# Attention of the first block: the values product of a differential unit ahead of the neighbourhood unit's two transpositions

## The chip, the cores and the metric

The kernel runs on one core of one Trainium2 chip. The metric is the device time of one execution in microseconds (us). The kernel before takes 4008.56 us (median of 3 runs, 4008.51 to 4011.54). Engine names in the profile: PE is TensorE's matmuls, PEld its weight loads, DVE is VectorE, ACT is ScalarE, POOL is GpSimd, SP is SyncE, which issues the DMAs.

## The reference, cut to what matters

Two transformer blocks run one after the other, of two layers each, on 512 tokens of width 1024. The change touches the first block only, in its two layers. Each layer of the first block mixes tokens in four ways, and two of them are attentions over 4 heads each:

```python
def diff_core(q, k, v, lam):
    s = jnp.einsum('bhcqd,bhckd->bhcqk', q, k).astype(jnp.float32) * (DIFF_QK ** -0.5)
    a = jax.nn.softmax(s, axis=-1)
    w = (a[:, :, 0] - lam * a[:, :, 1]).astype(v.dtype)
    return jnp.einsum('bhqk,bhkd->bhqd', w, v)
```

This is the differential attention: two softmaxes for a head, and the values are weighted by their difference. The neighbourhood attention (`na_attention_latent`) has one softmax per head, over a window of near tokens with a bias and over 256 context tokens, and then the same product with values. In layer 0 the 256 context tokens are queries too; their rows attend to the 256 context keys alone.

## The kernel before, in words

**Units.** `att_units` (L909) cuts a layer's attention into units of 128 queries and two softmaxes each. A differential unit ("diff") is one head with its two score maps; a neighbourhood unit ("na") is a pair of heads. They come in threes: diff of head 0, diff of head 1, then na of the group before. Layer 0 has 36 units, layer 1 has 24. Queries of kind "lat" have 768 keys (6 blocks of 128), queries of kind "ctx" 256 keys (2 blocks).

**What a unit needs.** Scores on PE (L1056) into PSUM banks 0 to 3; for na-lat units a bias by DVE (L1192) and a copy by ACT (L1292); the row extreme by DVE (L1203); the exponential by ACT (L1301), followed by a read of its row sum under the same line; then the weights: for a diff unit one DVE instruction (L1184) and a diagonal matrix by POOL (L1372), for an na unit two scalings by ACT (L1285). Next the weights are transposed on PE, blocks 0 to 2 into bank 4 and blocks 3 to 5 into bank 5 (L1071 for diff, where the transposition is a matmul with the diagonal, L1073 for na). DVE copies bank 4 to SBUF and ACT copies bank 5 (L1211 and L1310, into HC for diff and HL for na). A diff unit has one transposition, since its two maps are already joined; an na unit has two, `turn(u, 0)` and `turn(u, 1)`, and both use banks 4 and 5. For na-ctx units the first uses bank 4 alone and the second bank 5 alone. Last comes the product with values (`values`, L1091) into bank 6, which ACT copies out (L1317). A pair of diff units has one such product, with the second of them; an na unit has its own.

**The order.** Each engine has one written order. All engines run a software pipeline over steps `s`: step `s` issues the scores of unit `s`, the transposition of unit `s - 1` and the values of unit `s - 2`. "Beside" work goes into some steps as well (`item`, L1111): the Fourier and gated mixers of the layer (L1103, L1139, L1146, L1147, L1129) and modulation products (L399, L413). ACT's order inside a step matters here:

```python
if 1 <= s <= n and units[s - 1][1] == "na":
    take(s - 1, 0)          # ACT's copy of bank 5, first transposition
if s < n:
    exponential(s, 1)       # what scores(s + 1) waits for
```

Ahead of these lines ACT does `scaled(s - 1)` and `exponential(s, 0)`; after them the items, `mixed(s - 2)` (the copy of bank 6) and `take(s - 1, 1)`. DVE's order is: weights of `s - 1`, bias and row extremes of `s`, `take(s - 1, 0)` from bank 4, the items, `take(s - 1, 1)`.

**Waits on PE.** `turn(u, a)` waits for its weights (`soft_a ... "w"` for na) and for the copy that last emptied its bank (`turned_before`, L941). `values(u)` waits for both copies of its unit's transposed weights (L1081). `scores(s + 1)` waits for both exponentials of unit `s` (`scores_taken`, L925).

Of the kernel before, what the change touches and what calls it, by code (L numbers as in the profile page):

```python
# [165 lines left out]
def program(nc, d):  # L166
    ctx = ExitStack()
    with ctx:
# [45 lines left out]
        def C(name):  # L214
            a, n = CONST_AT[name]
            return cst[:, a:a + n]
# [6 lines left out]
        def bank(i):  # L223
            return ps[:, i, :]
# [164 lines left out]
        def tensor_mod_parts(e, w, li, i, pr, *free):  # L389


            w.wait_ge(silu_a.at(), silu_g.at(), *free)
            for b in range(2):
                wt = ada_buf(li, i + b)
                w.wait_ge(ada_landed(li, i + b))
                for r in range(2):
                    for q in range(4):
                        k = 4 * r + q
                        mm = e.matmul(pr[32 * q:32 * q + 32, 256 * b:256 * b + 256], silp[:, k, :], wt[:, k * 256:k * 256 + 256],  # L399
                                      start=r == 0, stop=r == 1)  # L400
                mm.then_inc(*mod_mm.up(li, i + b, "part"))
# [7 lines left out]
        def tensor_mod_sum(e, w, li, i, pr, *free):  # L409

            w.wait_ge(mod_a.at(li, i), (in_const, 16), *free)
            for j in range(4):
                mm = e.matmul(pr[:, 2 * j:2 * j + 2], modp[:, i // 2 % 2, 128 * j:128 * j + 128], C("sel"), start=True, stop=True)  # L413
            mm.then_inc(*mod_mm.up(li, i))
# [222 lines left out]
        def unit_of(l, kind, j=0):  # L637
            return next(p for p, u in enumerate(proj_units(l)) if u[0] == kind and u[2] == j)
# [5 lines left out]
        def pt_ready(l, kind, t):  # L644
            return lin_a.at(l, unit_of(l, kind), t // 2 * 2)
# [263 lines left out]
        def att_units(l):  # L909


            qts = [(i, "lat") for i in range(4)] + ([(i, "ctx") for i in range(2)] if l == 0 else [])
            groups = [(jt, *q) for jt in range(2) for q in qts]
            out = []
            for g in range(len(groups) + 1):
                if g < len(groups):
                    out += [(groups[g][0], "diff", hh, *groups[g][1:]) for hh in range(2)]
                if g:
                    out.append((groups[g - 1][0], "na", None, *groups[g - 1][1:]))
            return out  # L920
# [10 lines left out]
        def turns_of(l, u, a):  # L931

            jt, sort, hh, qi, kind = att_units(l)[u]
            if sort == "diff" and a:
                return []
            return [(range(0, 3), 4), (range(3, 6), 5)] if kind == "lat" else [(range(0, 2), 4 + (hh or a))]

        def turned(l, u, a, bk):
            return (wt_v if bk == 4 else wt_a).at(l, u, a)
# [10 lines left out]
        def has_values(l, u):  # L950
            return att_units(l)[u][2] != 0
# [7 lines left out]
        def values_before(l, u):  # L959

            return max((x for x in range(u) if has_values(l, x)), default=None)
# [28 lines left out]
        def last_diff(l, j):  # L990

            return max(u for u, x in enumerate(att_units(l)) if x[0] == j - 2 and x[1] == "diff")
# [44 lines left out]
        def tensor_attend(e, w, l):  # L1037
            units = att_units(l)
# [37 lines left out]
            def values(u):  # L1076
                jt, sort, hh, qi, kind = units[u]
                if not has_values(l, u):
                    return
                vb, vk, col = ([0, 1, 2, 3, 4, 5] if kind == "lat" else [4, 5]), *(("dv", 256) if sort == "diff" else ("nv", 512))  # L1080
                for x in (u - 1, u) if sort == "diff" else (u,):  # L1081
                    w.wait_ge(*(turned(l, x, a, bk) for a in range(2) for _, bk in turns_of(l, x, a)))
                before = values_before(l, u)
                if l == 0:
                    w.wait_ge(*(sub_a.at(l, j, "ln", 1) for j in (2, 3) if last_diff(l, j) + 4 <= u + 2))
                w.wait_ge(rot_v.at(l, unit_of(l, "dk", 1), "sin") if before is None else pv_a.at(l, before))
                for x, b in enumerate(vb):
                    w.wait_ge(pt_ready(l, vk, b))
                    for a in range(2):
                        c = col + (2 * jt + a) * 64  # L1090
                        mm = e.matmul(bank(6)[64 * a:64 * a + 64, 0:128], PT[:, b, c:c + 64], WT[sort][a][:, x * 128:x * 128 + 128], start=x == 0,  # L1091
                                      stop=x == len(vb) - 1)
                mm.then_inc(*pv_mm.up(l, u))

            def four_part(op, part, f, some):
                tts, n, _ = four(l, part)
                key, off = ((op, l, 0), 0) if part == 0 else (("fc", l, 1), 0 if op == "fc" else 512)
                wt = ring_buf(key, 2048 if part == 0 else 1024)
                w.wait_ge(landed(key))
                for x, t in enumerate(tts):  # L1100
                    if x in some:
                        w.wait_ge(pt_ready(l, "f", t))
                        mm = e.matmul(bank(7)[:, 0:n], PT[:, t, f * 128:f * 128 + 128], wt[:, off + x * n:off + x * n + n],  # L1103
                                      start=x == 0, stop=x == len(tts) - 1)
                return mm

            def free7(it):
                x = bank7.index(it)
                w.wait_ge(beside_taken(l, bank7[x - 1]) if x else norm_a.at("inv", (l, "mix"), len(segs_of(0)) - 1))

            def item(it):  # L1111
                pr = bank(7)
                if it[0] == "half":
                    free7(it[1:])
                    four_part(*it[1:], (0, 1))
                if it[0] not in ON_BANK7:
                    return
                free7(it)
                if it[0] == "parts":
                    tensor_mod_parts(e, w, it[1], it[2], pr)  # L1120
                elif it[0] == "sum":
                    tensor_mod_sum(e, w, it[1], it[2], pr)
                elif it[0] == "sqs":
                    j = it[1]
                    w.wait_ge(sub_a.at(l, j, "sq"))
                    if l == 0:
                        w.wait_ge(pv_a.at(l, values_before(l, min(last_diff(l, j) + 2, len(units)))))
                    for out, c, d_ in sub_psum(l):
                        mm = e.matmul(out, C("b64"), sub_buf(l, j)[:, c:d_], start=True, stop=True)  # L1129
                    mm.then_inc(*sub_mm.up(l, j))  # L1130
                elif it[0] == "gm":
                    _, f, (a, b) = it
                    wt = ring_buf(("ws", l), 512)
                    w.wait_ge(landed(("ws", l)))
                    for g in (2 * f, 2 * f + 1):
                        for t in range(a, b):
                            w.wait_ge(loc_v.at(l, "v", t))
                            r0 = g % 2 * 64
                            mm = e.matmul(pr[r0:r0 + 64, (t - a) * 128:(t - a) * 128 + 128], PT[:, t, 768 + g * 64:768 + g * 64 + 64],  # L1139
                                          wt[:, g * 128:g * 128 + 128], start=True, stop=True)  # L1140
                    mm.then_inc(*loc_mm.up(l, *it))
                elif it[0] == "fp":
                    _, part, f = it
                    n = four(l, part)[1]
                    w.wait_ge(loc_a.at(l, "fc", part, f), loc_v.at(l, "fs", part, f, "out"))
                    e.matmul(pr[:, 0:n], C("cd"), LB[:, 0:n], start=True, stop=False)  # L1146
                    e.matmul(pr[:, 0:n], C("sd"), LB[:, 512:512 + n], start=False, stop=True).then_inc(*loc_mm.up(l, *it))  # L1147
                else:
                    four_part(*it, (2, 3) if it[1] == 0 else (0, 1)).then_inc(*loc_mm.up(l, *it))

            n = len(units)
            for s in range(len(plan)):
                if s < n:
                    scores(s)
                for it in plan[s]:
                    item(it)
                if 1 <= s <= n:
                    turn(s - 1, 0)
                if 2 <= s <= n + 1:
                    values(s - 2)  # L1160
                if 1 <= s <= n:
                    turn(s - 1, 1)
# [2303 lines left out]
```

## Time and profile before

| | |
|---|---|
| median of 3 runs | 4008.56 us (4008.51 to 4011.54) |
| the profiled execution: its time, its span | 4007.92 us, 4006.1 us |
| PE busy over the span | 97% |
| DVE, ACT, POOL busy | 44%, 36%, 29% |
| mean granted TensorE clock | 0.988 of full |
| attention of layer 0 | from about 209 to 405 us of the span |
| attention of layer 1 | from about 1259 to 1408 us |

The span is the time from the program's first to its last instruction; the execution's time is 1.8 us longer. PE has the largest busy share, and the chain of work that ended last lies on PE for 86% of the span.

### The profile page before, as it was taken

How to read it: one execution, taken by the hardware profiler on the slowest of the kernel's cores; microseconds unless marked ns; L12 is line 12 of the kernel's file. 1: busy time of each engine (PE TensorE's matmuls, PEld its weight loads, DVE VectorE, ACT ScalarE, POOL GpSimd, SP SyncE). 2: the span in 40 equal slices, each digit the busy share in tenths (PEclk: the TensorE clock that was granted, in tenths of full speed). 3: DMA queues.
4: the chain of work that ended last, by engine and by line, in shares of the span. 5: the costliest groups of instructions: out<-in, count | busy, mean ns of one | idle time of the engine just before them, and what ended most of it. 6: DMA issues, size and time to landing. Idle time of an engine off the chain costs nothing.

```text
span 4006.1 us, 60979 instructions
## 1 busy us (share of the span) xinstructions
PE 3886.2 (97%) x26104; PEld 3087.3 (77%) x26104; DVE 1748.8 (44%) x2693; ACT 1423.3 (36%) x2258; POOL 1153.7 (29%) x689
## 2 busy tenths in 40 slices
PE   8999999999999899999999999999999999999998
PEld 6966778888877578887677778788876777887886
DVE  3366332323354643435755423334358464234333
ACT  3256332322233643332343333333324433334332
POOL 0010121222211023331332235333323322353333
PEclk9989999999999999999999999999999999999999
DMA  5014132323211022222111022222221111232221
GB/s 216 32 53 156 64 121 94 123 91 104 89 57 51 22 87 95 90 90 79 50 57 39 23 80 99 98 95 93 92 74 58 38 39 39 91 104 85 95 100 68
DMA packets 61356, 323.55 MB, mean 81 GB/s; under 512 B 6176, under 2 KB 6304, under 8 KB 36256
## 3 DMA queue, kind: packets, MB, share of 16 engines
q1 hardware_dynamic: 61088, 319.65, 23.0%
q8 instruction: 207, 3.39, 0.3%
q14 instruction: 61, 0.50, 0.0%
HBM read 317.53 MB, written 2.10 MB: 80 GB/s over the span
## 4 chain that ended last, share of the span: by engine, by line
PE 86%; DVE 5%; issue 3%; ACT 3%; POOL 1%; DMA 1%; SPq 0%; DVEq 0%; POOLq 0%; ACTq 0%
PE ps L1557 52%; PE ps L1568 4%; PE ps L735 3%; PE ps L766 3%; PE ps L2625 3%; PE ps L2259 2%; PE ps L1056 1%; PE ps L3127 1%; PE ps L338 1%; PE ps L1091 1%; DMA adab<-in_wada 1%; PE ps L2700 1%; PE ps L2722 1%; PE ps L2720 1%; PE ps L1071 1%
## 5 line engine op out<-in xcount | busy, mean ns | idle before, releaser
L1949 DVE SCALAR_TENSOR_TENSOR ftmp<-ps,vec,ftmp 128x511 f32<-128x511 f32 (+2 forms) x440 | 301.6, 694 | 342.8 <-ACT ftmp L1903 224.7
L1529 POOL TENSOR_TENSOR PWL<-ring,PWH 128x1024 fp32r<-128x1024 f32 (+2 forms) x114 | 260.5, 2285 | 655.4 <-ACT PWH L1515 655.4
L1529 POOL TENSOR_TENSOR WL<-ring,WH 128x1024 fp32r<-128x1024 f32 (+3 forms) x102 | 227.5, 2230 | 574.0 <-ACT WH L1515 557.4
L1515 ACT ACTIVATE PWH<-ring 128x1024 fp32r<-128x1024 f32 (+2 forms) x216 | 211.5, 982 | 465.6 <-PE ps L1557 422.2
L1515 ACT ACTIVATE WH<-ring 128x1024 fp32r<-128x1024 f32 (+3 forms) x160 | 158.5, 993 | 578.9 <-PE ps L1557 545.4
L1557 PE MATMUL ps<-FH,WH 128*128 128x512 f32 x1008 | 308.1, 360 | 0.0
L1557 PE MATMUL ps<-FL,WH 128*128 128x512 f32 x1008 | 304.5, 356 | 0.0
L1557 PE MATMUL ps<-FH,WL 128*128 128x512 f32 x1008 | 303.4, 355 | 0.0
L1529 POOL TENSOR_TENSOR PW3L<-ring,PW3H 128x1024 fp32r<-128x1024 f32 (+2 forms) x90 | 204.3, 2270 | 253.3 <-ACT PW3H L1515 253.2
L1522 DVE TENSOR_TENSOR PWL<-ring,PWH 128x1024 fp32r<-128x1024 f32 (+2 forms) x102 | 125.3, 1230 | 347.7 <-ACT PWH L1515 347.5
L1557 PEld LDWEIGHTS ps<-FH,WH 128*128 128x128 f32 x1008 | 166.3, 188 | 38.8 <-issue 9.9
L1972 POOL TENSOR_TENSOR ftmp<-ftmp 128x512 f32<-128x512 f32 (+1 forms) x88 | 126.3, 1435 | 230.6 <-DVE ftmp L1949 230.3
L1557 PEld LDWEIGHTS ps<-FH,WL 128*128 128x128 f32 x1008 | 166.2, 188 | 28.8
L1557 PEld LDWEIGHTS ps<-FL,WH 128*128 128x128 f32 x1008 | 165.9, 188 | 27.8
L1515 ACT ACTIVATE PW3H<-ring 128x1024 fp32r<-128x1024 f32 (+2 forms) x106 | 104.1, 982 | 229.9 <-PE ps L1557 218.7
L1557 PE MATMUL ps<-FH,PWL 128*128 128x512 f32 x432 | 170.2, 394 | 0.0
L1557 PE MATMUL ps<-FL,PWH 128*128 128x512 f32 x432 | 169.3, 392 | 0.0
L1557 PE MATMUL ps<-FH,PWH 128*128 128x512 f32 x432 | 167.6, 388 | 0.0
L1522 DVE TENSOR_TENSOR WL<-ring,WH 128x1024 fp32r<-128x1024 f32 (+3 forms) x58 | 68.2, 1176 | 217.2 <-ACT WH L1515 217.1
L1954 DVE TENSOR_TENSOR AL<-ftmp,AH 128x512 fp32r<-128x512 f32 (+1 forms) x88 | 66.8, 759 | 211.7 <-ACT AH L1913 211.7
L1913 ACT ACTIVATE AH<-ftmp 128x512 fp32r<-128x512 f32 (+1 forms) x88 | 60.3, 686 | 265.9 <-POOL ftmp L1972 265.9
L1557 PE MATMUL ps<-AH,WH 128*128 128x512 f32 x494 | 150.9, 360 | 0.0
(625 smaller groups left out, 9864.0 us busy)
## 6 DMA issues: line engine op xcount, KB each, us to landing
ring<-in_wup SPq DMA_DIRECT2D x88, 1024.0 KB, 4.8
adab<-in_wada SPq DMA_DIRECT2D x56, 512.0 KB, 5.3
ring<-in_wgate SPq DMA_DIRECT2D x24, 1024.0 KB, 4.8
ring<-in_wdown SPq DMA_DIRECT2D x24, 896.0 KB, 4.7
ring<-in_win SPq DMA_DIRECT2D x18, 1024.0 KB, 4.8
ring<-in_wout SPq DMA_DIRECT2D x16, 1024.0 KB, 4.8
ring<-in_wada SPq DMA_DIRECT2D x14, 1024.0 KB, 4.9
ring<-in_wdown SPq DMA_DIRECT2D x12, 1024.0 KB, 5.0
```

Of the source, the lines that this page charges most:

```text
L735: mm = e.matmul(pr[:, c:c + n], ww[:, k, :], h[part][:, k, :], start=start, stop=stop)
L766: mm = e.matmul(out, x, ww[:, k, :], start=kk == 0 and n == 0, stop=kk == 7 and n == 2)
L1515: e.activation(wh, view, ACT.Copy).then_inc(*whi_a.up(L, n))
L1522: e.tensor_tensor(wl, view, wh.bitcast(F32), SUB).then_inc(*wlo_v.up(L, n))
L1529: e.tensor_tensor(wl, view, wh.bitcast(F32), SUB).then_inc(*wlo_g.up(L, n))
L1557: mm = e.matmul(out[:, c:c + h.shape[1]], ww[:, k, :], h, start=at == 0 and p == 0, stop=at == K - 1 and p == 2)
L1568: mm = e.matmul(outs[j][:, c:c + h.shape[1]], ww[:, k, :], h, start=k == order[0] and ww is ws[j][0] and part == 0, stop=k == order[-1] an ...
L1949: e.scalar_tensor_tensor(out=dst, in0=src, scalar=conv_cols(L, ch, a), in1=dst, op0=MUL, op1=ADD).then_inc(*(ffn_v.up(L, "tap", x, j, c) i ...
L1954: e.tensor_tensor(lo, z_slot(L, x, 0)[:, 0:N], hi.bitcast(F32), SUB).then_inc(*ffn_v.up(L, "low", x))
L1972: e.tensor_tensor(zg, zg, zv, MUL).then_inc(*ffn_g.up(L, x))
L2259: mm = e.matmul(bank(6), ww[:, k, :], t, start=k == 0 and i == 0, stop=k == 7 and i == 2)
L2625: mm = e.matmul(front_bank(what, pp), ww[:, k, :], h, start=k == 0 and x == 0, stop=k == 7 and x == 2)
```

## The change

In a step whose transposed unit is na and whose values unit is diff, PE's product with the values is issued ahead of `turn(s - 1, 0)` instead of between `turn(s - 1, 0)` and `turn(s - 1, 1)`. The same instructions are issued. The order of the other engines is as before.

```diff
                 for it in plan[s]:
                     item(it)
+                ahead = 2 <= s <= n and units[s - 1][1] == "na" and units[s - 2][1] == "diff"
+                if ahead:
+                    values(s - 2)
                 if 1 <= s <= n:
                     turn(s - 1, 0)
-                if 2 <= s <= n + 1:
+                if 2 <= s <= n + 1 and not ahead:
                     values(s - 2)
                 if 1 <= s <= n:
                     turn(s - 1, 1)
```

The condition holds in 11 steps of layer 0 (s = 5, 8, 11, ..., 35) and in 7 of layer 1 (s = 5, 8, ..., 23).

## Rows read from the trace of the kernel before

**Rows 1.** Windows, one per layer's attention: us, busy of each engine, clock, DMA.
```profile
core 0: us, PE busy (x) PEld busy (x) DVE busy (x) ACT busy (x) POOL busy (x), PEclk, DMA share, GB/s
209.00:409.00 200.00, 181.22 (x1394) 120.90 (x1394) 128.01 (x255) 116.05 (x275) 23.19 (x31) 0.91 0.28 104
1259.00:1409.00 150.00, 129.56 (x944) 88.73 (x944) 101.49 (x172) 89.18 (x189) 16.10 (x21) 0.93 0.12 44
```

**Rows 2.** Groups by line, na transpositions, layer 0 then 1: busy, mean ns | idle before.
```profile
L1073 PE MATMUL ps<-cst,ar 128*128 128x128 f32 x112 | 18.4, 295 | 2.8 <-ACT ar L1285 2.8
...
L1073 PE MATMUL ps<-cst,ar 128*128 128x128 f32 x96 | 15.9, 308 | 13.3 <-ACT ar L1285 11.9 <-DVE HL L1211 1.4
```

**Rows 3.** Timeline, layer 1, s = 8: start us, length us, engine, line, tiles, count [idle before].
```profile
1309.52 0.82 PE L1073 MATMUL ps<-cst,ar 128*128 128x128 f32 x6
...
1310.27 1.53 PE L1091 MATMUL ps<-HC,ar 128*64 128x128 f32 x24
1310.38 0.49 ACT L1310 ACTIVATE HL<-ps 128x384 f32<-128x384 f32 x1 [0.24 <-PE ps L1073]
1310.77 0.90 ACT L1301 ACTIVATE ar<-ps,small 128x768 f32<-128x768 f32 x1
1311.55 0.20 ACT L1301 ACTIVATION_READ_ACCUMULATOR ar<-ps,small 128x1 f32 x1
1311.73 0.88 PE L1073 MATMUL ps<-cst,ar 128*128 128x128 f32 x6
...
1312.32 0.56 DVE L1211 COPY HL<-ps 128x384 f32<-128x384 f32 x1 [1.71 <-PE ps L1073]
1312.54 1.56 PE L1056 MATMUL ps<-ar 32*128 32x512 f32 x8
1312.65 0.49 ACT L1310 ACTIVATE HL<-ps 128x384 f32<-128x384 f32 x1 [0.52 <-PE ps L1073]
```

**Rows 4.** Timeline, layer 0, s = 11: the exponential of a context unit.
```profile
277.25 0.47 ACT L1301 ACTIVATE ar<-ps,small 128x256 f32<-128x256 f32 x1
```

**Rows 5.** Timeline, layer 1, s = 23: PE waits for DVE's copy.
```profile
1394.66 0.88 PE L1073 MATMUL ps<-cst,ar 128*128 128x128 f32 x6 [2.28 <-ACT ar L1285]
...
1397.53 0.55 DVE L1211 COPY HL<-ps 128x384 f32<-128x384 f32 x1
...
1398.23 1.49 PE L1073 MATMUL ps<-cst,ar 128*128 128x128 f32 x6 [0.53 <-DVE HL L1211]
```

**Rows 6.** Timeline, layer 1, s = 17.
```profile
1360.26 0.47 ACT L1310 ACTIVATE HC<-ps 128x384 f32<-128x384 f32 x1
1361.64 1.24 PE L1073 MATMUL ps<-cst,ar 128*128 128x128 f32 x6 [2.18 <-ACT ar L1285]
1362.81 2.79 PE L1091 MATMUL ps<-HC,ar 128*64 128x128 f32 x24
1363.20 0.47 ACT L1310 ACTIVATE HL<-ps 128x384 f32<-128x384 f32 x1
1363.57 0.90 ACT L1301 ACTIVATE ar<-ps,small 128x768 f32<-128x768 f32 x1
1366.34 1.56 PE L1056 MATMUL ps<-ar 32*128 32x512 f32 x8
```

**Rows 7.** Windows around the start of that step's transposition; columns as in Rows 1.
```profile
1354.00:1361.00 7.00, 5.24 (x40) 3.20 (x36) 5.38 (x10) 4.22 (x12) 0.60 (x1) 1.00 0.02 5
1362.20:1365.20 3.00, 3.00 (x26) 2.67 (x26) 0.64 (x2) 2.35 (x6) 0.00 (x0) 0.50 0.00 0
```

**Rows 8.** Timeline, layer 1, s = 14.
```profile
1345.24 1.54 PE L1073 MATMUL ps<-cst,ar 128*128 128x128 f32 x6 [3.77 <-ACT ar L1285]
...
1347.20 0.90 ACT L1301 ACTIVATE ar<-ps,small 128x768 f32<-128x768 f32 x1
...
1349.77 1.56 PE L1056 MATMUL ps<-ar 32*128 32x512 f32 x8
```

**Rows 9.** Timeline, layer 0, s = 20, a context unit's two transpositions.
```profile
320.49 0.44 PE L1073 MATMUL ps<-cst,ar 128*128 128x128 f32 x2 [1.52 <-ACT ar L1285]
...
321.67 0.89 ACT L1301 ACTIVATE ar<-ps,small 128x768 f32<-128x768 f32 x1
...
324.19 1.20 PE L1056 MATMUL ps<-ar 32*128 32x512 f32 x4
```

## The prediction

> **What bounds the kernel now.** I read the page first: PE is busy 97% of the span and holds 86% of the chain that ended last, so only what PE waits for can be won, and whatever PE is made to wait for is lost. The change touches two stretches, together 350 us of 4006; in them PE is busy for 181.22 of 200 us and 129.56 of 150 us, at 0.91 and 0.93 of its clock [rows 1]. The groups by line say where PE idles ahead of the transpositions that the change moves: 2.8 us in layer 0 and 13.3 us in layer 1, nearly all for ACT's scaling L1285 [rows 2]. The timeline then shows two kinds of step. In a **packed** step PE goes from the first transposition to the product, to the second transposition, to the next scores without a pause [rows 3]. In a **waiting** step it stands for 1.5 to 3.8 us ahead of the first transposition, and then has the product still to do [rows 6, 8, 9]. Of the 18 changed steps five wait: s = 20 of layer 0 and s = 14, 17, 20, 23 of layer 1. Eleven are packed, all with a latent na unit: s = 5, 8, 11, 14, 23, 26, 29, 32 of layer 0 and 5, 8, 11 of layer 1. The last two are s = 17 and 35 of layer 0, with a context na unit.
>
> **What the change costs in a packed step.** Nothing is added or removed. The product takes 1.46 us from start to start (1310.27 to 1311.73), the scores begin 3.02 us after the first transposition [rows 3]. Before, that product covered two things: the emptying of banks 4 and 5 between the two transpositions, and ACT's copy of bank 5 with the exponential behind it, which the next scores need. After it, the first transposition starts some 1.40 us later (the step begins with the product; 1.46 less 0.06 that the shorter first transposition shows), and both follow uncovered.
>
> The first is the bank. DVE's copy starts 0.59 us after a transposition that follows a product (1311.73 to 1312.32) and takes 0.56 [rows 3]; from the end of such a copy to PE's start are 0.15 (1398.08 to 1398.23) [rows 5]. So the second transposition starts 1.30 after the first instead of 0.81: a pause of 0.49 us. With it the scores come at 1.40 + 1.30 + 0.81 = 3.51, which is 0.49 later. ACT's copy of bank 5 is ready before the second half needs it.
>
> The second is the exponential. ACT's copy starts 0.92 after the transposition, the exponential 0.39 after the copy, and it ends with its read 0.98 later (1310.77 to 1311.75) [rows 3]; with 0.15 to PE the scores start at 1.40 + 0.92 + 0.39 + 0.98 + 0.15 = 3.84 at the earliest, 0.82 later than 3.02. Where the next unit is a context unit, the exponential takes 0.47 in place of 0.90 [rows 4], and the bank decides with 0.49.
>
> Seven packed steps have a latent unit next (s = 5, 8, 23, 26 of layer 0; 5, 8, 11 of layer 1) and four a context unit (11, 14, 29, 32 of layer 0). At s = 23 of layer 0 a pause of 0.43, one of those in the 2.8 us [rows 2], takes up half, which leaves about 0.3. Sum of the losses: 6 x 0.82 + 0.3 + 4 x 0.49 = 7.2 us. PE runs on without a pause behind these steps, so I pass the loss on whole. Its lower bound is nothing but the bank in all eleven, 11 x 0.49 less 0.4 = 5.0 (if ACT's work is ahead of where these rows have it), its upper bound the whole cover lost, 11 x 1.46 = 16; I take the worked value, since each term is a row.
>
> **The page that speaks against it.** The trace shows the second transposition directly behind a DVE copy with PE idle 0.53 us [rows 5]. The Trainium skill (Perfetto Trace Analysis, Matmuls) says that independent matmul groups should rotate through different PSUM banks, so that emptying one lies beside the next group's matmuls; here the product in bank 6 was the rotation between two users of banks 4 and 5. That rule gives the sign of the packed steps and no figure; without it the sum is the same.
>
> **What it gains in a waiting step.** The product can start when ACT has copied the diff unit's weights. At s = 17 of layer 1 that copy ends at 1360.73, PE at 1360.88; 1.46 later, at 1362.34, the transposition starts, past the 1361.64 at which it began before. ACT's copy was at 1363.20 and now can't start before 1363.26; exponential, read and scores follow at 1363.65, 1364.63 and 1364.78, against 1366.34: 1.56 us won [rows 6]. That holds at full clock. Before, the clock fell from 1.00 to 0.50 (2.4 to 1.2 GHz) behind the pause of 2.18, and the product took 2.79 us in place of 1.53 [rows 3, 6, 7]. With a pause of 1.4 left, the fall may still come; then the product's end and the transposition run at the slow level (1.24 us and more for it) and about 0.6 is won. So 0.6 to 1.6, and I take 1.2. The step at s = 20 has the same pattern 16.5 us later: another 1.2.
>
> At s = 14 the exponential starts at 1347.20 behind ACT's own queue and stays there; the scores could start at 1348.33 against 1349.77: 1.4 [rows 8]. At s = 20 of layer 0 likewise, 321.67 + 0.98 + 0.15 = 322.80 against 324.19: 1.4 [rows 9]; context transpositions use a bank each, so nothing is lost there. At s = 23 the second transposition waits for DVE's copy at 1397.53, which stands behind DVE's own work: 0 [rows 5]. The gains: 2 x 1.2 + 1.4 + 1.4 = 5.2, between 4.0 and 6.4 (plus 0.4 at s = 23 if its transposition runs at full clock). The other two steps with context units (s = 17, 35) I cost at nothing: banks apart, no wait ahead.
>
> **Other queues.** DVE's copy of the first transposition moves 1.4 us later in a packed step, and with it an item behind it; the diff weights L1184 come some 0.5 to 1.1 later, which a score product and an item of 1 to 2 us on PE cover, except at s = 5 of layer 0, where I allow 0.2. ACT's copy of bank 6 comes earlier. POOL waits only for DVE's weights. SP's loads wait for items, which move by the same tenths, and no DMA is on the path here (share 0.28 and 0.12) [rows 1].
>
> **The sum.** 7.2 + 0.2 - 5.2 = +2.2 us on the profiled execution's 4007.92, so 4010.1. That execution lies 0.6 below the median 4008.56; from the median it would be 4010.8. I say 4010.5.
>
> **Rivals.** A: *the clock decides against the change*. Each packed step now has pauses of 0.49 and 0.33; if the clock falls to 1.2 GHz behind them, a product costs 2.79 - 1.53 = 1.26 more [rows 3, 6]. In all eleven that is 14 us, 4024; over the bound of a measurement from five falls on. For it: layer 0 already runs at 0.91 [rows 1], and behind the pause of 1.52 in rows 9 the clock fell too. Against: the pauses are half of the smallest in those rows. Chance 0.08.
> B: *the losses drown*. If a later pause on PE takes up what the packed steps lose (PE idles 18.8 and 20.4 us in the two stretches [rows 1]), only the gains stand: -5.2, so 4003. Against: the pauses follow from score products, which move along. Chance 0.15.
> C: *the change does nothing where it should*: the product isn't ready when PE idles, the waiting steps stay, the losses stand: +7.4, so 4016. Against: the copy it needs ends 0.9 us before the transposition starts [rows 6]. Chance 0.12.
> The forecast, gains and losses near each other, has 0.65.
>
> **How the numbers follow.** Forecast alone: losses 5.0 to 8, gains 4.0 to 6.8, so -1.8 to +4, and 1.5 for the spread of the runs: 4006 to 4014. With most of B and C: 4004 to 4016. A measurement can tell 0.2%, about 8 us, from no change: below 4000.5 is faster, above 4016.6 slower. Faster needs B with full gains and more: 0.03. Slower is A and the tail of C: 0.09. The same: 0.88.
>
> **What would show it.** Right: L1073's idle for L1285 in layer 1 falls from 11.9 to some 6 us; a new idle for DVE L1211 of about 0.49 stands ahead of ten or eleven second transpositions (5 us in all), and one for ACT L1301 of about 0.3 ahead of the scores in the latent packed steps; the layer 0 stretch grows by 3 to 4 us and layer 1's shrinks by 1 or 2. Wrong: if the scores of a packed step still start 3.0 us after its start, if the exponential isn't late, or if the granted clock of the two stretches falls below 0.91 and 0.93 [rows 1].

## The result, and the profile after

The changed kernel takes **4016.91 us** (median of 15 runs, 4010.47 to 4027.18). The kernel before, run beside it, takes 4005.96 (15 runs, 3998.20 to 4011.54). The ratio is 1.0027, with a 95% interval of 1.0020 to 1.0035: slower by 8 to 14 us. The forecast was 4010.5 with a range that ended at 4016. It missed: the change costs more than the range allowed for, and it lies beyond the 0.2% that I had called no change.

The page of the changed kernel: span, busy times, granted clock in 40 slices.

```profile
span 4015.0 us, 60976 instructions
...
PE 3888.9 (97%) x26104; PEld 3088.3 (77%) x26104; DVE 1751.1 (44%) x2693; ACT 1421.6 (35%) x2258; POOL 1152.8 (29%) x689
...
PEclk9989999999999999999999999999999999999999
```

The page alone tells nothing of the cause: the instructions are the same, and the shares too. The windows of the two stretches, and one inside the second; columns as in [rows 1]:

```profile
209.00:415.00 206.00, 182.91 (x1410) 121.91 (x1409) 128.83 (x255) 115.80 (x275) 23.13 (x31) 0.93 0.28 101
1265.00:1418.00 153.00, 131.89 (x944) 89.57 (x944) 102.66 (x172) 87.35 (x189) 15.99 (x21) 0.92 0.12 43
...
1406.00:1415.50 9.50, 7.85 (x42) 5.65 (x44) 1.12 (x2) 3.56 (x7) 0.00 (x0) 0.50 0.01 2
```

The windows are a little wider than those of [rows 1], so I measured both stretches from their first score product to the first weight product behind them. Layer 0 grew from 195.5 to 199.6 us and layer 1 from 147.8 to 151.4. I had expected layer 0 to grow by 3 to 4 and layer 1 to shrink by 1 or 2. That layer 0 comes near it is partly chance: in a second pair of traces (below) it grew from 192.6 to 198.4, and layer 1 from 146.2 to 147.9. The third row is a stretch at the end of layer 1 that ran wholly at 0.50 of the clock; before there were 3.4 us of that kind in the same place.

The groups by line, na transpositions (L1073) and the score products that wait (L1056), changed kernel, layer 0 and then layer 1. DVE's copy is now L1214, ACT's scaling L1288, the exponential L1304:

```profile
L1056 PE MATMUL ps<-ar 32*128 32x512 f32 x64 | 20.9, 729 | 7.4 <-ACT ar L1304 6.6 <-ACT ar L845 0.8
L1073 PE MATMUL ps<-cst,ar 128*128 128x128 f32 x112 | 17.1, 284 | 4.6 <-DVE HL L1214 3.3 <-ACT ar L1288 1.2
...
L1073 PE MATMUL ps<-cst,ar 128*128 128x128 f32 x96 | 16.6, 315 | 8.3 <-DVE HL L1214 5.0 <-ACT ar L1288 2.9 <-ACT HL L1313 0.3
L1091 PE MATMUL ps<-HC,ar 128*64 128x128 f32 x192 | 14.1, 302 | 5.1 <-issue 5.1
```

Against [rows 2]: the idle for ACT's scaling in layer 1 fell from 11.9 to 2.9, but 5.1 of it has only moved ahead of the product (L1091). New are the waits for DVE's copy, 3.3 us (eight times 0.41) in layer 0 and 5.0 in layer 1, where the old order had none and 1.4. The scores' wait for the exponential is 6.6 in layer 0 and was 4.0, as the same view of the kernel before shows:

```profile
L1056 PE MATMUL ps<-ar 32*128 32x512 f32 x64 | 20.6, 722 | 4.8 <-ACT ar L1301 4.0 <-ACT ar L845 0.8
```

The timeline of a packed step, changed kernel, layer 1, s = 8; it answers to [rows 3]:

```profile
1316.55 1.53 PE L1091 MATMUL ps<-HC,ar 128*64 128x128 f32 x24
...
1318.01 0.88 PE L1073 MATMUL ps<-cst,ar 128*128 128x128 f32 x6
1318.60 0.56 DVE L1214 COPY HL<-ps 128x384 f32<-128x384 f32 x1 [2.04 <-PE ps L1073]
1318.93 0.49 ACT L1313 ACTIVATE HL<-ps 128x384 f32<-128x384 f32 x1 [1.86 <-PE ps L1073]
...
1319.30 0.85 PE L1073 MATMUL ps<-cst,ar 128*128 128x128 f32 x6 [0.41 <-DVE HL L1214]
1319.31 0.90 ACT L1304 ACTIVATE ar<-ps,small 128x768 f32<-128x768 f32 x1
...
1320.10 0.20 ACT L1304 ACTIVATION_READ_ACCUMULATOR ar<-ps,small 128x1 f32 x1
...
1320.44 1.56 PE L1056 MATMUL ps<-ar 32*128 32x512 f32 x8 [0.29 <-ACT ar L1304]
```

Both pauses stand where they were forecast: 0.41 for the bank (forecast 0.49) and 0.29 for the exponential (forecast 0.33). From the first transposition to the scores it takes 2.43 us; I had 3.84 - 1.40 = 2.44. The rule of the Trainium skill (Perfetto Trace Analysis, Matmuls) on rotating PSUM banks agrees with this trace: the two transpositions now directly follow each other on the same banks, and 0.41 us of PE idle stand between them.

### The profile page after: what moved, and what is told of

Same layout as the page of the kernel before. It is cut to its first block, busy times and chain, and to the rows that moved or that the text cites. A ratio compares the mean times of both kernels' runs of the same rounds, so it can differ in the third digit from the quotient of the medians.

```text
span 4015.0 us, 60976 instructions
## 1 busy us (share of the span) xinstructions
PE 3888.9 (97%) x26104; PEld 3088.3 (77%) x26104; DVE 1751.1 (44%) x2693; ACT 1421.6 (35%) x2258; POOL 1152.8 (29%) x689
## 4 chain that ended last, share of the span: by engine, by line
PE 86%; DVE 5%; issue 3%; ACT 3%; POOL 1%; DMA 1%; SPq 0%; DVEq 0%; POOLq 0%; ACTq 0%
PE ps L1560 52%; PE ps L1571 4%; PE ps L735 3%; PE ps L766 3%; PE ps L2628 3%; PE ps L2262 2%; PE ps L1056 2%; PE ps L3130 1%; PE ps L338 1%; PE ps L1091 1%; DMA adab<-in_wada 1%; PE ps L2703 1%; PE ps L2725 1%; PE ps L2723 1%; PE ps L1071 1%
```

## The experiments

Each was timed beside the kernel before on the same chip. The runs of one kernel spread widely (the kernel before: 3997 to 4019 us around 4006.6), so no median settles a term of 1 us. What settles it is the time from one step's score products to the next step's, read from the trace of each kernel, with the time at 1.2 GHz inside in brackets. (Other steps are left out. s = 21 of layer 0 and s = 15 of layer 1 are not changed themselves; each follows a changed step.)

```
us (of these at 1.2 GHz)
step     before      before 2    after       after 2     e1_packed   e8_swap     e6_between  e9_before_fill
L0 s=8    6.33 (0)    6.33 (0)    7.30 (0)    7.30 (0)    7.30 (0)    6.94 (0)    6.14 (0)    6.33 (0)
L0 s=11   5.81 (0)    5.82 (0)    6.42 (0)    6.42 (0)    6.43 (0)    6.42 (0)    6.10 (0)    5.82 (0)
L0 s=14   8.34 (3.4)  6.64 (0)    8.90 (3.4)  8.89 (3.4)  8.83 (3.4)  8.89 (3.4)  8.38 (3.4)  6.65 (0)
L0 s=20   7.84 (3.2)  6.45 (0)    6.45 (0)    6.45 (0)    7.81 (3.2)  7.88 (3.4)  6.45 (0)    6.45 (0)
L0 s=21   4.67 (0.2)  4.57 (0)    6.11 (3.4)  6.10 (3.4)  4.70 (0.2)  4.60 (0)    4.57 (0)    4.57 (0)
L1 s=8    6.33 (0)    6.33 (0)    7.30 (0)    7.30 (0)    7.30 (0)    6.94 (0)    6.14 (0)    6.33 (0)
L1 s=14   9.86 (3.4)  9.97 (3.4)  8.38 (0)    8.38 (0)   10.59 (6.8) 10.55 (6.8) 10.83 (6.8)  8.41 (0)
L1 s=15   4.82 (0)    4.82 (0)    4.57 (0)    6.09 (3.4)  4.82 (0)    4.82 (0)    4.71 (0)    4.82 (0)
L1 s=17   8.43 (3.4)  8.43 (3.4)  8.38 (3.4)  6.95 (0)    8.40 (3.4)  8.43 (3.4)  6.82 (0)    6.82 (0)
L1 s=20   8.56 (3.4)  6.95 (0)    8.17 (3.4)  6.95 (0)    6.95 (0)    6.95 (0)    8.54 (3.4)  6.95 (0)
tail     16.56 (3.4) 16.23 (3.4) 19.81 (10.2) 17.51 (3.4) 16.2 (3.4)  16.3 (3.4)  16.2 (3.4)  16.00 (0)
```

"Before 2" and "after 2" are a second execution of each of the two kernels (below); the tail runs from the scores of s = 23 in layer 1 to the first weight product, L437.

**Half of the change: the packed steps alone.**

```diff
-                ahead = 2 <= s <= n and units[s - 1][1] == "na" and units[s - 2][1] == "diff"
+                ahead = s in ((5, 8, 11, 14, 23, 26, 29, 32), (5, 8, 11))[l]
```

> The product goes ahead in the eleven packed steps alone (s = 5, 8, 11, 14, 23, 26, 29, 32 of layer 0 and 5, 8, 11 of layer 1). Both theories: the scores behind each latent packed step come about 0.96 us later (0.3 at s = 23 of layer 0) and behind each of the other four about 0.6, in all 8.0 us, so 1.0020 of the kernel before. T1 (waits only): the changed kernel's other seven steps then give something back, and this kernel is slower than the changed one. T2 (clock): those seven give nothing or cost, and this kernel is faster than the changed one by 1 to 4 us.

Measured: 4012.20 against 4006.24, ratio 1.0017 (1.0008 to 1.0026), so 3 to 10 us slower. The packed steps of its trace are those of the changed kernel to 0.01 us, apart from s = 14 and 23 of layer 0 (0.07 and 0.03 us shorter) and s = 32, where the clock fell in this trace and not in that one. The changed kernel had 1.0027 in its own comparison, so the other seven steps seem to cost something and not to give back; the two intervals overlap, so the times alone don't show it.

**The other half: the waiting steps alone.**

```diff
+                ahead = s in ((20,), (14, 17, 20, 23))[l]
```

> The product goes ahead in the five waiting steps alone (s = 20 of layer 0; 14, 17, 20, 23 of layer 1). T1 (waits only): 4 to 5 us faster than before, as the forecast's gains had it (0.9988). T2 (the clock falls on what is left of the pauses and the moved product no longer keeps it up): 0 to 3 us slower than before, since s = 17 and 20 give 0.1 to 0.4 each in the trace of the changed kernel and s = 23 costs some 3.

Measured: 4004.11 against 4006.24, ratio 1.0000 (0.9991 to 1.0010). The gain of 5.2 is not there. Its trace has 6.12 (3.4) at s = 21 of layer 0, 8.38 (0) at s = 14 of layer 1, 8.32 (3.4) and 8.22 (3.4) at s = 17 and 20, and 19.75 us with 10.2 at 1.2 GHz in the tail.

**The last waiting step alone.**

```diff
+                ahead = (l, s) == (1, 23)
```

> The product goes ahead in one step alone, s = 23 of layer 1. T1 (waits only): no difference, at most 0.5 us faster, since the second transposition waits for DVE's copy either way. T2 (clock): 2 to 4 us slower than before; a longer stretch at half clock lies over the last transpositions and products of layer 1.

Measured: 4008.32 against 4006.24, ratio 1.0009 (1.0000 to 1.0018); its tail takes 17.44 us against 16.2 to 16.6 of the old order. I had costed this step at nothing. The timeline of the changed kernel shows why (TensorE, layer 1, s = 23 and behind it):

```profile
1400.14 1.53 PE L1091 MATMUL ps<-HC,ar 128*64 128x128 f32 x24 [1.50 <-issue]
1401.60 0.88 PE L1073 MATMUL ps<-cst,ar 128*128 128x128 f32 x6
1404.52 0.85 PE L1073 MATMUL ps<-cst,ar 128*128 128x128 f32 x6 [2.05 <-DVE HL L1214]
...
1406.83 1.54 PE L1073 MATMUL ps<-cst,ar 128*128 128x128 f32 x6 [1.45 <-ACT ar L1288]
1408.30 2.83 PE L1091 MATMUL ps<-HL,ar 128*64 128x128 f32 x24
1411.95 1.51 PE L1073 MATMUL ps<-cst,ar 128*128 128x128 f32 x6 [0.82 <-DVE HL L1214]
```

The product no longer lies between the two transpositions, so PE has three pauses within 8.2 us (1.50, 2.05, 1.45; the old order has 2.28 and 0.53 at that step, [rows 5]), and from 1405.6 on all that follows runs at 1.2 GHz, up to 1415.8.

**Work against the pauses.** The suspicion was now that the waiting steps' time hangs on the clock and not on the order. To test it PE gets matmuls in its pauses whose result nobody reads. `busy(k)` issues k of them, each two records of the trace and some 0.94 us (three take 2.84).

```diff
+            def busy(k):
+                w.wait_ge(sub_a.at(1, 2, "ln", 0))
+                for _ in range(k):
+                    e.matmul(bank(7), C("ident"), C("cos1"), start=True, stop=True)
...
+                if l == 1 and s in (17, 20, 23):
+                    busy(3)
```

Here and at s = 24 three, and four ahead of the second transposition of s = 23, on top of the changed kernel:

> The changed kernel with idle PE time of layer 1's last steps filled by extra matmuls of 128x128 by 512 columns into bank 7, whose result nobody reads: 3 ahead of the product at s = 17, 20 and 23, 4 between the two transpositions of s = 23, 3 ahead of the first of the last unit and 1 ahead of its second (17 in all, 0.43 us each by L1147 in the trace). T1 (waits only): no better than the changed kernel, up to 1 us slower. T2 (clock): no stretch at half clock there, and 5 to 7 us faster than the changed kernel.

(The edit has 16 of them, not 17: none stands ahead of the last unit's second transposition.)

Measured: 4015.87 against 4006.24, ratio 1.0020 (1.0010 to 1.0031). From s = 14 of layer 1 to the end of its stretch the clock held, but the test was spoilt by its size: three take 2.84 us, and s = 17 takes 8.16 us where it takes 6.95 with the clock up and none added. So a second one, on top of the changed kernel, with one at s = 17, 20, 23, 24, one behind the product of s = 14 and two between the transpositions of s = 23:

> As the run with 17 extra products, which turned out to be two matmul instructions each (2.84 us for three of them) and to delay the real product by 1.28 us; now few enough to end before the real work is ready: 1 ahead of the product at s = 17, 20, 23 of layer 1, 1 ahead of the first transposition at s = 14, 2 between the two of s = 23, 1 ahead of the last unit's (0.94 us each). T1 (waits only): like the changed kernel. T2 (clock): no half clock in layer 1's attention behind its first microseconds; at s = 17 and 20 the next scores begin 1.5 us earlier than before, 5.3 us after the end of the last scores; the stage of layer 1 is 5 to 7 us shorter than in the changed kernel (151.4), the time 5 us under it.

Measured: 4014.59 against 4007.63, ratio 1.0015 (1.0004 to 1.0026). The layer 1 stretch is 144.8 us (151.4 and 147.9 in the two traces of the changed kernel), with s = 17 at 6.81, s = 20 at 6.95 and a tail of 16.00. The losses of the packed steps remain. The ratio is 0.0012 under the changed kernel's 1.0027, near the expected 5 us, but the intervals overlap.

**Other work as the cover.** In the packed steps the product goes ahead, and the step's items, which PE has to do anyway, go between the two transpositions:

```diff
-                for it in plan[s]:
-                    item(it)
+                if s not in between:
+                    for it in plan[s]:
+                        item(it)
+                if s in ahead or s in between:
+                    values(s - 2)
                 if 1 <= s <= n:
                     turn(s - 1, 0)
+                if s in between:
+                    for it in plan[s]:
+                        item(it)
```

> In the eleven packed steps the order is product, first transposition, beside items, second transposition (before: items, transposition, product, transposition); all other steps as before. T1 (the product covered the emptying of banks 4 and 5 and ACT's copy; items of 1 to 3 us cover it as well): no pause for DVE's copy or the exponential, and the pauses ahead of the items (1.97, 1.04, 0.89, 0.82, 0.68, 0.27 in the trace of before) shrink: 4 to 8 us faster than before. Rival (what costs is the later first transposition itself, through DVE and ACT): 3 to 8 us slower than before, as the packed steps alone were.

Measured: 4004.07 against 4007.63, ratio 1.0000 (0.9988 to 1.0011); the expected gain is not there. The timeline of TensorE, layer 1, s = 8, in this kernel:

```profile
1307.75 1.53 PE L1091 MATMUL ps<-HC,ar 128*64 128x128 f32 x24
1309.21 0.88 PE L1073 MATMUL ps<-cst,ar 128*128 128x128 f32 x6
1309.92 1.88 PE L1103 MATMUL ps<-ring,ar 128*128 128x512 f32 x4
1311.64 0.82 PE L1073 MATMUL ps<-cst,ar 128*128 128x128 f32 x6
1312.39 1.56 PE L1056 MATMUL ps<-ar 32*128 32x512 f32 x8
```

Both pauses of the changed order are gone (6.14 us for the step, against 7.30 and 6.33). The cover can thus be replaced. But in other steps the item had also covered the time until ACT had copied the product's weights, and the pause now stands ahead of the product: 0.75 us at s = 11 of layer 0 (6.10 us for the step, 5.81 before), 0.71 at s = 26 (7.22 and 6.43) and 2.25 at s = 32, where the clock stayed down for 6.8 us (9.86 for the step; 7.24 before, with a fall, and 6.08 without). So layer 0 takes 197.7 us (195.5 and 192.6 in the two traces of before) and layer 1 146.2 (147.8 and 146.2), and the steps give back what the others won. The 6.8 us at 1.2 GHz at s = 14 of layer 1 aren't of this edit, which leaves that step alone: they stand in e1_packed and e8_swap too.

**That order, with the waiting steps ahead as well** (s = 20 of layer 0; 14, 17, 20 of layer 1, without 23):

```diff
+            between = ((5, 8, 11, 14, 23, 26, 29, 32), (5, 8, 11))[l]
+            ahead = ((20,), (14, 17, 20))[l]
```

> The order of the run before this one in the packed steps, and the product ahead in the waiting steps s = 20 of layer 0 and 14, 17, 20 of layer 1 (not 23). T1 (waits only): 3 to 5 us faster than the run before this one. T2 (clock takes back what the waiting steps win): within 1.5 us of the run before this one.

Measured: 4009.14 against 4007.63, ratio 1.0004 (0.9993 to 1.0015). The gain of 3 to 5 us isn't there: it is 5 us above the run before this one by the medians and 1.6 by the ratios, with intervals that overlap. Its layer 1 stretch is short, 142.7 us, and its layer 0 stretch 197.8, together 340.5 (343.3 and 338.8 in the two traces of before), yet the whole is not faster. Its profiled execution took 4015.69, so that one lost its time outside the two stretches, where 48.9 us ran at 1.2 GHz and 43.1 in the first trace of before. I can't tell more from it.

**The exponential taken by itself.** As in the packed steps alone, and ACT does the exponential ahead of its copy of bank 5 (`late` moves the call behind or ahead of it):

```diff
-                if 1 <= s <= n and units[s - 1][1] == "na":
+                late = units[s - 1][1] == "diff" or s in ((5, 8, 11, 14, 23, 26, 29, 32), (5, 8, 11))[l] if 1 <= s <= n else None
+                if late is False:
```

> The packed-only kernel with ACT's exponential of the next unit put ahead of its copy of bank 5 in those steps. If the exponential behind that copy is what makes the latent packed steps lose 0.96 and not 0.6, the pause ahead of the next scores (0.29, for ACT L1301's read) goes in the seven latent steps and each loses 0.6; the pause of 0.42 ahead of the second transpositions stays. Rival (only the bank counts): no change, 0.96 each.

Measured: one execution, 4011.25. The timeline of layer 1, s = 8, in this kernel:

```profile
1311.47 1.53 PE L1091 MATMUL ps<-HC,ar 128*64 128x128 f32 x24
...
1311.88 0.89 ACT L1304 ACTIVATE ar<-ps,small 128x768 f32<-128x768 f32 x1
...
1312.93 0.88 PE L1073 MATMUL ps<-cst,ar 128*128 128x128 f32 x6
...
1314.22 0.85 PE L1073 MATMUL ps<-cst,ar 128*128 128x128 f32 x6 [0.41 <-DVE HL L1214]
...
1315.01 1.56 PE L1056 MATMUL ps<-ar 32*128 32x512 f32 x8
```

The exponential now lies beside the product and the scores follow without a pause. The step takes 6.94 in place of 7.30, so the exponential is 0.36 of the 0.97 lost, and 0.61 stay with the bank; the steps with a context unit next, where the bank alone decides, lose the same 0.61 with or without it (L0 s = 11). This is one trace, but steps without a fall repeat to 0.01 us in the two traces of either kernel.

**The kernel before with products in its pauses, in its own order.** Two at s = 14, 17, 20 and 23 of layer 1 ahead of the first transposition, one at s = 24:

```diff
+                if l == 1 and s in (17, 20, 23, 24):
+                    busy(1 if s == 24 else 2)
+                ahead = False
...
+                if (l, s) == (1, 14):
+                    busy(2)
```

> The kernel before, its order untouched, with extra products of 0.94 us each in PE's pauses of layer 1's last steps: 2 ahead of the first transposition at s = 14, 17, 20, 23 and 1 ahead of the last unit's. T2a (the order wins nothing where the clock is up; all of a waiting step's gain was the comparison of a product at half clock with one at full clock): at s = 17 and 20 the next scores begin 5.3 us after the last ones end, as they do in the changed kernel with extra products (5.26, 5.39), against 6.88 and 7.0 before; layer 1's stage is 141 to 143 us (147.8 before); the time 3 to 6 us under the kernel before. T1 (the order wins 1.5 us in each even at full clock): 6.8 us there and a stage of 146 or more.

Measured: 4000.42 against 4006.57, ratio 0.9989 (0.9978 to 1.0000). This is the run that decides. The order is that of before, and s = 14 and 17 still come down from 9.86 and 8.43 to 8.41 and 6.82; at s = 17 the next scores begin 5.26 us after the last ones end, as expected if the order wins nothing in the step. The window over s = 15 to 24 and the timeline of s = 17 in this kernel:

```profile
1345.00:1399.00 54.00, 49.22 (x402) 32.98 (x402) 37.08 (x64) 35.79 (x79) 3.63 (x6) 1.00 0.00 1
```

```profile
1354.66 1.99 PE L1154 MATMUL ps<-cst 128*128 128x512 f32 x4
1356.90 0.88 PE L1073 MATMUL ps<-cst,ar 128*128 128x128 f32 x6 [0.26 <-ACT ar L1297]
1357.72 1.53 PE L1091 MATMUL ps<-HC,ar 128*64 128x128 f32 x24
1359.18 0.88 PE L1073 MATMUL ps<-cst,ar 128*128 128x128 f32 x6
```

The clock is 1.00 throughout; the product takes 1.53 where it took 2.79 [rows 6]. The layer 1 stretch is 142.9 us, 4.9 less than in the first trace of before and 3.3 less than in the second.

**The same with the waiting steps ahead** (s = 20 of layer 0; 14, 17, 20 of layer 1), one product each at 14, 17, 20 and 24, two at 23:

```diff
+                if l == 1 and s in (17, 20, 23, 24):
+                    busy(2 if s == 23 else 1)
+                ahead = s in ((20,), (14, 17, 20))[l]
```

> The product ahead only at s = 20 of layer 0 and 14, 17, 20 of layer 1, with extra products in the pauses that are left (1 at s = 14, 17, 20, 2 at s = 23, 1 ahead of the last unit's). T2a: the same stage of layer 1 as the run before this one within 0.7 us, 5.3 us between the scores. T1: 3 to 4 us shorter than the run before this one.

Measured: 4002.06 against 4006.57, ratio 0.9984 (0.9972 to 0.9996); layer 1 143.5 us. Both are faster than the changed kernel, and than the one before, the first of them at the edge of its interval. Between their times the runs show no difference. The traces show a small one: this run has one fall, at s = 15 of layer 1 (6.04 us in place of 4.57), and where neither has a fall the product ahead saves nothing in the waiting step itself and 0.25 us in the step behind it.

**Both kernels once more**, unchanged, one execution each.

> The kernel before again, for a second look at where the clock falls in its attention stages. T2 (falls depend on where the pauses lie): falls behind the pauses of L1073 at s = 14, 17, 20, 23 of layer 1 again, within one of the first trace's four, and both stages within 3 us of 195.5 and 147.8.

> The changed kernel again. If the step costs are of its order and not of chance, the gaps ahead of the second transpositions (0.42) and the scores (0.29) repeat to 0.02 us; stage lengths within 3 us of 199.6 and 151.4, the clock half at the tail of layer 1 again.

Measured: 4001.21 and 4016.15. The packed steps repeat to 0.01 us where the clock is the same in both traces, and so do the pauses of 0.41 and 0.29. For the kernel before, the falls came at three of the four places and the stretches (192.6 and 146.2) lie within 3 us, as expected. For the changed one, layer 0 does (198.4), but layer 1 takes 147.9 and not 151.4, with 3.4 us at 1.2 GHz in its tail and not 10.2. The falls of the clock do not repeat: s = 14, 20 and 29 of layer 0 and s = 20 of layer 1 in the kernel before, s = 17 and 20 of layer 1 in the changed one, ran at full clock this time, and the changed one fell at s = 15 of layer 1 instead. The kernel before, layer 1, s = 20, TensorE:

```profile
1370.59 1.56 PE L1056 MATMUL ps<-ar 32*128 32x512 f32 x8
1374.46 0.88 PE L1073 MATMUL ps<-cst,ar 128*128 128x128 f32 x6 [2.31 <-ACT ar L1285]
1375.27 1.53 PE L1091 MATMUL ps<-HC,ar 128*64 128x128 f32 x24
1376.73 0.88 PE L1073 MATMUL ps<-cst,ar 128*128 128x128 f32 x6
1377.54 1.56 PE L1056 MATMUL ps<-ar 32*128 32x512 f32 x8
```

## Why the prediction was wrong, step by step

**The losses of the packed steps: right in mechanism; in sum too, partly by luck.** Forecast 7.4 us (7.2 and 0.2). The eleven steps of the two first profiles differ by 0.66, 0.97, 0.61, 0.56, 0.33 and 0.82 (L0 s = 5 to 26), 0.54 (s = 29), 0.03 (s = 32) and 0.96, 0.97, 0.96 in layer 1: 7.4 us. (For s = 29 and 32 the value before is one of the same order at full clock, 5.71 and 6.08; at s = 14 both had a fall.) Four of the seven latent steps lose 0.97 and not 0.82, which makes up for s = 5 (0.66 for 0.82 and 0.2) and s = 32. The bank and the exponential were as worked out; the 0.06 that I had set off for a shorter transposition isn't saved, and the product starts 0.09 later behind the item than the transposition did. The single steps were less alike than my two classes: s = 32 lost nothing, since PE waited for ACT there in the old order too. The packed steps alone confirm the sum (ratio 1.0017, about 6.8 us).

**The gains of the waiting steps: the step that failed.** "0.6 to 1.6, and I take 1.2", twice, and 1.4 twice: 5.2 us. At equal clock the gain in these steps is **0**, and 0.6 us in all in the steps behind them. The rows had it. At full clock the old order needs 3.02 us from the first transposition to the scores [rows 3], so from 1361.64 the scores of s = 17 would have come at 1364.66. The new order brings them, by my own working, at 1364.78. I compared that with 1366.34, a number that held a product at 1.2 GHz, and took the difference of the clock for a gain of the order. The mechanism is the same one that I had counted in the packed steps: the product ahead starts 0.8 us earlier than the transposition could, and the bank and exponential laid bare behind it cost just that. At s = 20 of layer 0, where the transpositions share no bank, it is the exponential alone: the pause of 1.52 us ahead of the first transposition [rows 9] became one of 1.47 ahead of the next scores. The traces show it at full clock in both orders: 6.45 and 6.45 (L0 s = 20), 8.41 and 8.38 (L1 s = 14), 6.95 and 6.95 (s = 20). Only the step behind each waiting step of layer 1 gains, 4.57 in place of 4.82 us: a pause of 0.27 ahead of its transposition, for DVE's weights, is gone (at s = 16 a part of that, 0.13, is given back).

What remains is the clock. In its first trace the changed order leaves a pause of 1.36 us in place of 2.18 at s = 17 and of 1.50 in place of 2.28 at s = 23, and the clock fell all the same. The timeline of the changed kernel, TensorE, layer 1, s = 17, answers to [rows 6]:

```profile
1365.17 1.56 PE L1056 MATMUL ps<-ar 32*128 32x512 f32 x8
1368.09 2.83 PE L1091 MATMUL ps<-HC,ar 128*64 128x128 f32 x24 [1.36 <-issue]
1370.85 1.14 PE L1073 MATMUL ps<-cst,ar 128*128 128x128 f32 x6
1372.41 0.85 PE L1073 MATMUL ps<-cst,ar 128*128 128x128 f32 x6 [0.42 <-DVE HL L1214]
1373.55 1.56 PE L1056 MATMUL ps<-ar 32*128 32x512 f32 x8 [0.29 <-ACT ar L1304]
```

The product again takes 2.83. The falls must be counted over the steps behind as well, for some only moved there. At s = 20 of layer 0 no trace with the new order has a fall, but six of seven have one at s = 21, behind the pause that the order put ahead of the scores. The changed kernel there, first the timeline of TensorE, then a window from 1.0 us behind that pause, columns as in [rows 1]:

```profile
327.10 0.84 PE L1073 MATMUL ps<-cst,ar 128*128 128x128 f32 x4
329.42 2.02 PE L1056 MATMUL ps<-ar 32*128 32x512 f32 x8 [1.47 <-ACT ar L1304]
```

```profile
330.38:333.79 3.41, 3.41 (x13) 2.40 (x10) 2.34 (x3) 1.40 (x3) 0.00 (x0) 0.50 0.00 0
```

Each waiting step with the two steps behind it, over all traces without added products in that layer:

```
us, mean (traces)    old order, falls     new order, falls     both at full clock
L0 s=20 to 22        15.5 (7), in 3       16.2 (7), in 6       14.9 and 14.9
L1 s=14 to 16        18.4 (6), in 6       16.7 (4), in 1       16.5 and 16.4
L1 s=17 to 19        16.0 (6), in 5       15.6 (4), in 3       14.8 and 14.6
L1 s=20 to 22        15.7 (6), in 3       15.3 (4), in 2       14.9 and 14.6
```

(The 16.5 is of the kernel with added products, e9_before_fill; no other has the old order there without a fall.) The gain is 1.8 us on average, and not 5.2: 0.6 of it is the order's and the rest is clock, 1.6 won at s = 14 of layer 1 and 0.7 lost in layer 0. These are few traces, so the share of the clock is rough.

**The tail, costed at 0 and up to 0.4 won: wrong in sign.** It costs 1.2 us where the clock falls once and 3.3 where it stays down for 10.2 us. At full clock it takes 16.00 us in either order; only the kernels with added products show that.

**A step costed at 0 that costs a little.** s = 35 of layer 0: from its scores to the first weight product it takes 9.29 us at full clock in the new order and 9.03 in the old.

**The sum.** Losses 7.4, waiting steps -1.8, tail +2.3 (18.6 us on average in the four traces with the new order at s = 23, 16.3 in six with the old one), s = 35 +0.3: 8.2 us, against a forecast of 2.2 and a measured 8 to 14. The stretches give a like sum another way. Four traces have layer 0 wholly in the old order (192.5 to 195.5 us, mean 193.3) and four wholly in the changed one (198.4 to 202.5, mean 200.1); layer 1 takes 147.0 in the two traces of before and 149.7 in the two of after. That is 6.8 + 2.7 = 9.5 us, inside the interval.

The 6.8 of layer 0 is 1.3 more than its steps account for (4.5 packed, 0.7 at s = 20 to 22, 0.3 at s = 35), and that is the clock. Ahead of s = 14's item stands a pause of 1.97 us for ACT, in both orders alike, and the step has a fall in 2 of 6 traces with the old packed order and in 8 of 8 with the product moved (8.4 to 8.9 us in place of 6.6, where I have counted 0.56). But at s = 29 it is 3 of 6 and 0 of 8, and at s = 32 5 of 6 and 6 of 8. From s = 5 on the four old traces have 5, 2, 2 and 2 falls in layer 0, the four changed ones 3, 2, 4 and 4. So the change moves falls; whether it makes more of them in layer 0 these traces don't show, and no run was made to test it.

**The rivals.** C came nearest: the losses stand whole and the waiting steps give almost nothing, 4016. Its reason was wrong, though: the product was ready, and PE did start it early (the idle for the scaling fell to 2.9, not 6). A, that the clock decides, was right about the cause and wrong about the place: in none of the packed steps' traces did the clock fall directly behind a pause of 0.41 or 0.29; it fell in the tail, at s = 21 of layer 0, and more often at s = 14 there. (At the waiting step s = 14 of layer 1 it fell in two traces, r_after and e10_wait_fill, 1.0 and 1.3 us behind the last of four pauses: 1.49 in the one and 0.43 in the other, then 0.43, 0.26 or 0.25, and 0.42.) Its argument against, that the new pauses are half of the smallest with a fall, rested on the rows alone: the same trace has falls at pauses of 1.04 and 0.89 us, at s = 29 and 32 of layer 0. B is refuted by the packed steps alone.

## What to carry to other kernels

Compare two orders of the same work only at the same granted clock: if a row of the old order ran at 1.2 GHz, work out first what it would take at 2.4, for otherwise the clock's gain is booked to the edit. Count the steps behind an edit as well, since a fall can move there. Work that separates two users of a buffer is a cover and has a price when it moves, even in a step where PE waits anyway; here moving it ahead of waits of 1.5 to 3.8 us bought nothing in the waiting steps themselves. Where pauses of 1.5 to 3.8 us on PE can't be removed, matmuls whose result nobody reads may be worth more than any reordering (here 0.9989 and 0.9984 of the time, where the reordering gave 1.0027), and they must end before the awaited data come.

## What the runs showed of the hardware

The clock fell behind pauses of 1.36 and 2.18 us in a stretch where PE was otherwise busy, and not behind one of 2.31 us in the rows of s = 20 above; the same kernel in the same place fell in one execution and not in another. It fell at a shorter one as well, in the second execution of the kernel before (TensorE, layer 0, s = 32), where matmuls that take 1.93 us at full clock took 3.53:

```profile
379.87 3.53 PE L399 MATMUL ps<-ring,silp 128*32 128x256 f32 x32 [0.89 <-DVE small L420]
```

A fall of 3.4 us cost its step 1.1 to 1.7 us, in the tail of the old order 0.2 to 0.6; in the tail of the changed order the clock stayed down for 10.2 us in two of four traces. What tells a pause that brings a fall from one that doesn't stays open. In the four kernels with matmuls in the pauses (e4_fill, e5_fill2, e9_before_fill, e10_wait_fill) one fall was left from s = 14 of layer 1 to the end of the stretch; the kernel before has four and three there in its two traces.
